# Prompt attention: scaling the probabilities of local and compressed keys on VectorE or on GpSimd

## The reference, cut to what matters

```python
def masked_softmax(s, valid):
    s = jnp.where(valid, s, NEG)
    m = jnp.max(s, axis=-1, keepdims=True)
    e = jnp.where(valid, jnp.exp(s - m), 0.0)
    return e / jnp.maximum(jnp.sum(e, axis=-1, keepdims=True), TINY)
...
return jnp.einsum('bthg,bthgd->bthd', gates.astype(o3.dtype), o3)   # the three sparse outputs, gated
```

## Time and profile before

| what | value |
|---|---|
| time of the runs, median of 3 | 1444.11 us (1442.19 to 1448.04) |
| time of the profiled execution | 1449.1 us |
| its span | 1447.0 us |
| PE busy | 1304.1 us, 90% |
| DVE busy | 693.3 us, 48% |
| ACT busy | 405.0 us, 28% |
| POOL busy | 237.3 us, 16% |

### The profile page before, as it was taken

One profiled execution on the slowest core, in us unless ns is written; L12 is line 12 of the kernel. 1 busy time (PEld: TensorE's weight loads), 2 busy tenths in 40 slices (PEclk: granted clock), 3 DMA queues, 4 the chain that ended last, 5 costly groups with the idle time before them and its releaser, 6 DMA issues.

```text
span 1447.0 us, 19519 instructions
## 1 busy us (share of the span) xinstructions
PE 1304.1 (90%) x6942; PEld 782.1 (54%) x6942; DVE 693.3 (48%) x1565; ACT 405.0 (28%) x858; POOL 237.3 (16%) x273
## 2 busy tenths in 40 slices
PE   3699999999999999878998999999937999999966
PEld 1468787777877555546666656544422333333322
DVE  5526574675744111256565553344762344433329
ACT  2232231422322010135655664222200111111016
POOL 0003021031211000212222222000001222211132
PEclk9799999999999999969999999999957999999988
DMA  9802020130201204306000002520057987595856
GB/s 305 247 26 59 17 73 1 31 59 17 72 2 46 95 9 79 99 12 167 25 21 5 1 1 84 161 80 30 29 199 248 316 287 258 177 319 158 291 177 225
DMA packets 123237, 163.18 MB, mean 113 GB/s; under 512 B 29763, under 2 KB 98547, under 8 KB 123160
## 3 DMA queue, kind: packets, MB, share of 16 engines
q1 hardware_dynamic: 108840, 112.75, 25.5%
q0 software_dynamic: 14320, 49.41, 9.8%
HBM read 225.01 MB, written 36.45 MB: 181 GB/s over the span
## 4 chain that ended last, share of the span: by engine, by line
PE 74%; DVE 16%; POOL 4%; DMA 2%; issue 2%; ACT 2%; SPq 0%; DVEq 0%; POOLq 0%; ACTq 0%
PE act L652 15%; PE vec L1159 11%; PE vec L919 9%; PE vec L681 7%; PE vec L702 4%; POOL arena L2204 3%; DVE arena L1795 3%; PE act L877 3%; PE vec L853 3%; PE act L865 3%; PE act L1172 2%; PE vec L1172 2%; PE vec L817 1%; DMA arena<-x_rows,arena 1%; PE vec L662 1%
## 5 line engine op out<-in xcount | busy, mean ns | idle before, releaser
L652 PE MATMUL act<-arena 128*128 128x352 f32 x768 | 239.1, 467 | 0.4 <-issue 0.4
L652 PEld LDWEIGHTS act<-arena 128*128 128x128 f32 x768 | 145.5, 193 | 77.0 <-issue 3.6
L1159 PE MATMUL vec<-arena 128*64 128x512 f32 x768 | 174.0, 605 | 2.6 <-issue 2.6
L1795 DVE CUSTOM_DVE_ANT_0 arena<-vec,arena 128x128 f32<-128x128 f32 (+9 forms) x200 | 86.8, 459 | 102.7 <-PE vec L853 92.8
L919 PE MATMUL vec<-arena 128*128 128x512 f32 (+1 forms) x288 | 127.8, 599 | 0.4 <-ACT arena L1357 0.4
L1159 PEld LDWEIGHTS vec<-arena 128*64 128x64 f32 x768 | 54.6, 138 | 105.2 <-issue 104.9
L681 PE MATMUL vec<-arena 128*128 128x512 f32 (+1 forms) x256 | 99.9, 546 | 0.0
L1370 ACT COPY arena<-act 128x512 f32<-128x512 f32 (+11 forms) x176 | 63.7, 431 | 105.1 <-PE act L865 105.1
L2204 POOL TENSOR_SCALAR arena<-arena 128x640 f32<-128x640 f32 (+4 forms) x64 | 59.2, 937 | 189.8 <-DVE arena L1807 189.8
L2089 DVE TENSOR_SCALAR arena<-arena 128x256 f32<-128x256 f32 x24 | 7.1, 296 | 172.4 <-ACT arena L1468 172.4
L853 PE MATMUL vec<-arena 64*128 64x512 f32 (+11 forms) x352 | 86.0, 486 | 3.2 <-DVE arena L1795 2.0
(11 more groups left out here) (379 smaller groups left out, 1902.3 us busy)
## 6 DMA issues: line engine op xcount, KB each, us to landing
arena<-in_exp_w SPq DMA_DIRECT2D x144, 1024.0 KB
y_rows<-arena POOLq DMA_DIRECT2D x48, 256.0 KB, 4.9
arena<-in_w_in SPq DMA_DIRECT2D x16, 512.0 KB, 7.1
arena<-in_x_prompt SPq DMA_DIRECT2D x8, 512.0 KB, 10.3
x_spill<-arena POOLq DMA_DIRECT2D x8, 512.0 KB, 6.0
arena<-x_spill SPq DMA_DIRECT2D x8, 512.0 KB, 5.5
arena<-in_cache_fox_kv SPq DMA_DIRECT2D x16, 256.0 KB, 3.5
x_rows<-arena POOLq DMA_DIRECT2D x8, 512.0 KB, 2.9
```

Of the source, the lines that this page charges most:

```text
L652: last = mm(bk[:, 0:n], W[k % 2][:, c, m * P:(m + 1) * P], xT[:, c, a:a + n], start=c == 0, stop=c == NC - 1)
L1159: last = mm(gu_bank[p][o], xgT[p][:, c, o], Wgu[:, slot, c, :], start=c == 0, stop=c == NC - 1)
L1795: ins = e.tensor_tensor_reduce(out=s[:, a + o:a + o + w], in0=bk[:, o:o + w], in1=bias, scale=1.0, scalar=prior, op0=ALU.add, op1=ALU.min, ...
```

## The change

The scaling of the odd steps' tiles moves from GpSimd's loop into DVE's `normalise`, directly behind the reciprocal, as even steps had it. GpSimd's loop keeps only the decay tiles. The widths are the same: `unit_keys(kind, i)[1]` is (i + 1) x 128 for `fox` and `slc`.

```diff
@@ DVE, normalise(d)
             e.wait_ge(*E.own())
             e.reciprocal(sm_[:, 2:4], sm_[:, 2:4]).then_inc(*E.done(("factors", d)))
-            if d % 2 == 0:
-                e.wait_ge(*E.own())
-                L = (i + 1) * P
-                for j in range(2):
-                    s = score_tiles(d)[j][:, 0:L]
-                    ts(s, s, sm_[:, 2 + j:3 + j], None, ALU.mult).then_inc(*E.done(("probs", d)))
+            e.wait_ge(*E.own())
+            for j, kind in enumerate(kinds):
+                s = score_tiles(d)[j][:, 0:unit_keys(kind, i)[1]]
+                ts(s, s, sm_[:, 2 + j:3 + j], None, ALU.mult).then_inc(*E.done(("probs", d)))
@@ GpSimd, stage attn, loop over PAIRS
             if d % 16 == 9 and h + 1 < H:
                 e.wait_ge(*E.at(("cumf", h + 1)))
                 tt(foxdiag[(h + 1) % 2], cumf[(h + 1) % 2].rearrange("p (t k) -> p t k", t=8), C["diagmask"].unsqueeze(1).to_broadcast([P, 8, P]), ALU.add).then_inc(*E.done(("foxdiag", h + 1)))
-            if d % 2:
-                e.wait_ge(*E.at(("factors", d)))
-                for j, kind in enumerate(kinds):
-                    s = score_tiles(d)[j][:, 0:unit_keys(kind, i)[1]]
-                    e.tensor_scalar(s, s, small[:, d % 4, 2 + j:3 + j], None, ALU.mult).then_inc(*E.done(("probs", d)))
```

## The result

The changed kernel takes 1421.04 us (median, 1419.92 to 1422.19) beside 1443.69 for the kernel before: a ratio of 0.9838, 95% interval 0.9815 to 0.9861. In a second comparison on another chip (e5) it is 0.9862 (0.9839 to 0.9884). So 20 to 23 us faster; forecast were 1424 us and 20.0 us less.

A forecast was written before the change was run, and what follows sets the result against it. PE, 90% busy, was taken as the bound, held up by GpSimd's scaling latency. Gaps 12.0 plus clock 8.0 give 20.0 us, taking the profiled 1449.1 to 1429.1, less 5.0 to the runs' median: 1424 us, range 1415 to 1436.

The forecast's parts named there:

- Latency, not load: Attention stage, odd steps: GpSimd's scaling latency, not its load, holds up PE's transposes, 18.3 us of waits in 24 pieces.
- The cost on DVE: 64 scalings add 21 us to DVE, 551 ns per 640 columns, covered by idle gaps ahead of odd scores.
- The gaps of PE: PE's waits for odd-step scalings: 18.3 us, all closing but those of i = 3; 12.0 us saved.
- the 0.13 a head: At i = 1, 0.13 us of PE's 0.84 gap was to stay in each of four heads, 0.5 in all.
- The decay tile at i = 3: First three heads: GpSimd's decay tile starts first and blocks DVE's scaling of d = 7; PE 0.4 us later each.
- the row of before: Old blocked DVE pair, 2.76 us at 724.89: read as released 1.65 us after the decay tile's start, making PE 0.2 later.
- sum by the rule for the three places: At i = 3 in three heads, DVE blocked for GpSimd's whole instruction: 3 x 0.9 = 2.7 us rather than 1.2.
- The clock: PE's half-clock stretches in the attention stage: five of seven go with closed gaps, 1.6 us each, saving 8.0 us.
- No collision at i = 3: Rival: the decay tile doesn't hold DVE's scaling, so i = 3 gaps close and two more drops go; 1415 us, chance 0.08.
- Waits go, clock stays: Rival: PE's gaps close but as many half-clock drops remain; 1432 us, chance 0.17.
- DVE the bound: Rival: DVE's gaps before odd scores vanish, so scalings delay scores; 8 us slower, 1452 us, chance 0.05.
- something else last: Rival: ACT's copies or late DVE scores hold PE instead, giving back 6 to 8 us; about 1439 us, chance 0.10.

The follow-up runs named there:

- e5: The changed kernel run once more, unaltered, on another chip: 1422.49 us, ratio 0.9862 to the kernel before.
- e2: Against the kernel before, only the odd steps of i = 5, 6 and 7 scaled by DVE, the others still by GpSimd: ratio 0.9982.
- e3: Against the kernel before, only the odd steps of i = 2 and i = 4 scaled by DVE: ratio 0.9934.
- e4: Changed kernel, with DVE also multiplying each odd-step tile by 1.0 before scaling it: 1426.46 us, ratio 0.9901 to the kernel before.
- e1: Changed kernel, with GpSimd forming the next head's decay tile only once DVE has scaled d = 8: ratio 0.9816 to the kernel before.
- e8: The kernel before, unaltered, profiled once more in one execution: stage 262.3 us, no ratio given.
- e6: The kernel of e1 run again beside the changed kernel on one chip: 1410.97 us, ratio 0.9786 to the kernel before.
- e7: The kernel of e6, with the first head's decay tile formed in two parts, first 128 columns first: 1416.04 us, ratio 0.9801 to the kernel before.
- e10: The kernel before, with only the decay tile delayed until DVE has scaled d = 8: ratio 1.0001.
- e9: Changed kernel, but the odd steps of i = 3 stay with GpSimd in all four heads: ratio 0.9852 to the kernel before.
- e11: Against the kernel before, only the odd steps of i = 0 and i = 1 scaled by DVE: ratio 0.9970.

## Why the prediction was right, step by step

**Latency, not load.** Right. GpSimd was idle for most of the stage, and moving 24 scalings (e2) won less than moving 16 (e3). What counts is the way from the reciprocal to the end of the scaling, 2.4 us on GpSimd and 0.74 on DVE at i = 5 (730.20 to 730.94).

**The cost on DVE.** Right: 554 ns for 640 columns (551 forecast), 225 to 251 ns for the compressed parts (bound 286). DVE's busy time rose from 693.3 to 712.4 us, 19 for the 21, with 5 us of blocking in it and 5 us of the old blocking out. It is covered by the gaps ahead of the odd scores, as said; e4, with 15 us more of it, bears that out.

**The gaps of PE.** 12.0 us forecast, 18.7 - 6.0 = 12.7 measured. At i = 1 the 0.13 a head did not appear: DVE goes from reciprocal to scaling in 0.03 us, not the 0.09 that GpSimd took, and the pair takes 0.50 for 0.53. A gap of 0.37 at i = 7 of the last head was not foreseen: it is the last even step, whose transposes now reach DVE's scaling of 1024 columns before it is done.

**The decay tile at i = 3.** Right in its mechanism: it starts first, DVE is held, PE starts 0.17 to 0.23 us later than before in the three heads, the 0.2 of the row and not the 0.4 that I took. The uncontested pair takes 0.64 (e1), so DVE was let go at 711.90 + 2.21 - 0.64 = 713.47, 1.79 us after the start of a tile of 2.00 and 0.21 before its end. But the prediction misread the row of before. The pair of 2.76 us at 724.89 is two operations:

```profile
724.89 0.56 DVE L1813 TENSOR_SCALAR arena<-arena 128x640 f32<-128x640 f32 x1
725.36 2.29 DVE L1813 TENSOR_SCALAR arena<-arena 128x640 f32<-128x640 f32 x1
```

The first started ahead of the decay tile (724.98, 2.33 us) and took its usual time; only the second was held. Less its own 0.55 it was let go at 727.10, not 726.63: 2.12 us after the tile's start, not 1.65, and again 0.21 before its end. That the forecast of 0.2 came out was partly luck: the 1.65 was too short, but the tile took 2.00 after the change, where no scaling ran ahead of it, so the hold was 1.79, and the pair took 0.64 for the 0.73 assumed.

The Trainium skill ("SBUF — State Buffer", section "SBUF: two separate sides") has the pair of ports locked for the whole instruction. Both kernels' traces agree but for the last 0.2 us of GpSimd's record; the prediction had taken the release to be earlier than that. The prediction's sum by the rule for the three places, 2.7 us, was four times the measured 0.6, in part because it reckoned with a tile of 2.33 us.

**The clock.** This term was too large for the traces: 8.0 us for five drops, and it was 4 x 1.6 = 6.4, seven drops to three. Five went as forecast, and i = 3 of the third head, which had none in the first trace, got one. e8 shows that the count of seven is steady and the places are not, so "five of the seven stand behind gaps that close" rested on one draw. What holds is the rule behind it: a drop comes behind a gap, and not behind each. In e1, e6 and e7, whose longest gaps after the ramp are 0.70 us (PE waiting for a PSUM bank ahead of the decay rows, once in each of three heads in all the traces), there is none.

The clocks of the single runs don't tell 6.4 from 8.0. By an estimate from them, twice the missing share of the clock times the span, the nine runs of the kernel before on the chip of e5 spent 157 us at half clock in the whole execution (155 and 156 on the two other chips), the four of e5 146 and the four of the first comparison 140. That is 11 to 17 us less, worth 5 to 8 at 1.6 us for a stretch of 3.4.

**The sum.** 12.7 + 6.4 = 19.1 for the 20.0, against 20 to 23 measured. The two profiled executions differ by 27.5 us, more than the medians: 3.4 is the ramp at the start, about 2 is older than the stage (the first decay tile starts at 628.53 and at 626.51), 1.7 lies behind it. Carrying over the 5.0 us by which the first profile lay above the median was right. What is left of the first comparison, some 3 us, is about the ramp's size, and the second comparison gives 20. Nothing shows that the ramp is long more often with the kernel before: among traces in which GpSimd scales the first odd steps it was long in two of five (before and e8, not e2, e3 and e10), among those in which DVE does, in two of six (e6 and e9, not the changed kernel, e1, e5 and e11; e4 and e7 change more), and it is settled before these steps (e8).

**Rivals.** "No collision at i = 3" was priced at 5.9 + 3.2 = 9.1 us; made true by an edit of its own it gives 9.0 in the stage. The sum agrees better than its parts: the gaps gave 4.7 for 5.9 and the clock 4.8 for 3.2, three drops for two. "Waits go, clock stays" (1432) falls with the measured 1421 and 1422.5 and with the drops, seven to three in both traces of the changed kernel. "DVE the bound" did not come, nor did "something else last", but for the 0.37 us named above.

## What to carry to other kernels

An engine that is 16% busy can hold the bound engine up: compare the way from the producer to the waiting engine with the slack there, turn by turn, before asking how busy anyone is. Price a move to another engine by the idle gaps that stand in its order at that place, and look which operation of the engine that was relieved now starts earlier and what it meets; here one wait, which puts the decay tile where DVE reads PSUM, was worth another 11 us, and the kernel of e6, at 0.9786, is the fastest of those run. And where the clock drops behind idle gaps, a gap costs more than its length: 0.8 us lost could cost 2.4.

## What the runs showed of the hardware

- GpSimd's multiplication by a column factor took 1884 ns for 128x640 in float32, DVE's 554 in the same place.
- DVE's multiplication of 128x640 by the constant 1.0 took 495 ns (e4), by a factor of each row 554.
- A DVE scaling that starts behind a GpSimd operation of two inputs waits for nearly all of it (pair 2.21 us for 0.64), until 0.21 us before its end in both kernels, and the GpSimd operation took 2.33 for 2.00 us where a DVE scaling had started 0.09 ahead of it; DVE's score operations, which read PSUM and one tile of SBUF, ran beside the same GpSimd operation in e1 and slowed neither (2.00 us for GpSimd).
- Idle gaps of PE of 0.8 us in a stage that is otherwise dense are followed by a stretch of over 3 us at 1.2 GHz about every second time: the first trace of the kernel before has 14 gaps of 0.79 us or more in its dense part and seven drops, its second again seven, at partly other places. In the three traces whose longest gaps are 0.70 us there was none. A drop costs 1.6 us.
